# Query and key projections on sixteen 32x32 tiles of TensorE, and another order of work within each mLSTM head

## The chip, the cores and the metric

One core of a Trainium2 chip. The metric is the device time of one execution of the whole program, in microseconds (us). 1% is some 20 us.

## The reference, cut to what matters

Two decoder layers for a prompt of 512 tokens and 64 sample tokens (8 sequences of 8). Layer 0 mixes with an RG-LRU, layer 1 with an mLSTM, and each is followed by a SwiGLU and a gated input embedding. Only the mLSTM's heads are touched. For each of 4 heads of width 512:

```
q = block_diag(xc, w_q); k = block_diag(xc, w_k) * 512 ** -0.5; v = block_diag(xm, w_v)    # blocks of 4x4
S   = (q k^T) * exp(decay, causal)
num = inter * (q C) + S v ;  den = inter * (q n) + sum(S) ;  h = num / max(|den|, exp(-m))
C_new = scale * C + kw^T v ;  n_new = scale * n + sum(kw)       # C is 512x512 for each head and sequence
h = rms_norm(h) ; y = (sigmoid(o_pre) * h) @ w_out
```

C of the 8 sample sequences is read and written once for each head: 8 MB in and 8 MB out.

## The kernel before, in words

Most of the program is the function `job` (L2105): weights of 256x256 are loaded (SP), split in two halves of precision (ACT L929, POOL L634) and multiplied on TensorE (L2125). Between the mLSTM's input and output products lies the stage of the heads, without any `job`, where this change is made.

Everything in that stage is written out by hand: each engine has its own list of steps, and semaphores join them. TensorE's pieces and the PSUM bank of each are listed in `head_order` (L71); `take` (L2252) waits on TensorE until the last user of a bank has emptied it, `done` counts pieces. The engines run their lists strictly in order.

The pieces of one head on TensorE:
- `projection` (L2284, L2288): q and k of the prompt, 4 fp32 products each of 128x128 weights, which are block-diagonal in blocks of 4, with 512 columns. Each takes one bank, which ACT copies out (L1235, L1241). `sample_projection` (L2296): the same for 64 sample tokens, pieces `qs` and `ks`.
- `value` (L2281), pieces `v0` to `v4`; `value_stack` (L2305, `vs`) and `sample_key_rows` (L2326, `st`): rows of v and k, for the updates of C.
- `unit(h, u)`, u from 0 to 7: for 4 sequences and 128 rows of C, q C on four column tiles of 128x32 (L2376), then the update's product on four row tiles of 32x128 (L2386) into banks 4 to 7. DVE's `update` (L1917, L1924) adds it to C in place, and SP stores that. The loop on SP (L566) stores half a unit, and then loads one six halves ahead, as soon as the store before has landed; six halves of C have room.
- the scores `sc0`, `sc13`, `sc2s` (L2340, L2362), the key rows `r0` to `r3` (L2334), `weighted` `pv0` to `pv3` (L2398), `den` and `ds` (L2407 to L2418), `prompt_state` `cp0` to `cp3` (L2426), the square sums `hp` of the prompt and `hn` of the samples (L2454).
- `numerators` (L2429): `cn`, 4 products with one column, and `nt`, 12 products with 32 or 64 columns (L2443, L2445).

In heads 1 to 3 the order before is: qs, ks, vs, v0, hn of the head before, v1, v2, st, v3, v4, q, unit 0, k, unit 1, sc0, unit 2, sc13, sc2s, unit 3, r0 to r3, unit 4, pv0, pv1, unit 5, pv2, pv3, unit 6, den, ds, cp0, cp1, unit 7, hp, cp2, cp3, cn, nt.

The rows with the decay of head h+1 are spread over all partitions by five transfers (`spread_rows`, L546), which SP issues after the store of v = 13, that is the second half of unit 6. DVE turns them into exponents (`decay_exponents(h+1)`, L1862) after `update(h, 7)`, waiting for the transfers, and ACT takes the exponential (`exps_`, L1279) ahead of emptying cp2, cp3, cn and nt. `inverses` (L1959) is DVE's reciprocal. After head 3, ACT starts to split the weights of the next `job`, and SP issues them after all stores of the heads.

## Time and profile before

| | us |
|---|---|
| median of 3 runs | 2048.03 |
| lowest and highest | 2043.64, 2049.47 |
| the profiled execution, its own time | 2048.11 |
| its span, first to last instruction | 2046.4 |

2048.11 - 2046.4 = 1.7 us lie around the span. TensorE is busy for 95% of the span. The granted clock of TensorE was 0.968 of 2.4 GHz on average; it has two levels, 2.4 and 1.2 GHz, and a clock of 0.50 in a row means 1.2. Each fp32 product appears as two records of MATMUL, and each lasts longer than its step to the next, since they overlap: a step is read from one start to the next.

### The profile page before, as it was taken

The page shows a single profiled execution, that of the slowest core. Times are in us where ns is not written, and L with a number is a line of the kernel's source. Part 1 is how long each engine was busy: PE and PEld are TensorE (multiplying, and loading weights), DVE is VectorE, ACT ScalarE, POOL GpSimd, SP SyncE. Part 2 cuts the span into 40 slices and gives each one's busy share as a digit, 9 for nine tenths or more (in the row PEclk, how much of TensorE's full clock was granted, in tenths as well). Part 3 has the DMA queues.
Part 4 walks back from the last instruction along what each step waited for, and adds up shares of the span by engine and source line. Part 5 has one row for each costly group of instructions (what it writes and reads, how often), then busy time and mean ns, then how long its engine had stood idle before and what let it go on. Part 6 is the DMA issues. An engine that isn't in the chain of part 4 may idle for free.

```text
span 2046.4 us, 35519 instructions
## 1 busy us (share of the span) xinstructions
PE 1943.5 (95%) x13511; PEld 1798.8 (88%) x13511; DVE 722.6 (35%) x848; ACT 736.4 (36%) x1086; POOL 811.3 (40%) x659
## 2 busy tenths in 40 slices
PE   6999899999999989899889999999999999999997
PEld 5999899999999989897454665799999999999996
DVE  5677622111111122676646466421222111111213
ACT  3576633322222234434242334241443312212332
POOL 4243364553553545562100100263655545545432
PEclk7999899999999999999879889899999999999998
DMA  3232132222222223221649467322233222222212
GB/s 110 72 93 78 57 99 78 82 83 83 82 82 83 82 68 76 81 82 62 227 142 306 164 237 231 129 89 72 72 89 86 83 89 75 82 90 76 84 60 74
DMA packets 187003, 209.43 MB, mean 102 GB/s; under 512 B 24459, under 2 KB 150035, under 8 KB 186847
## 3 DMA queue, kind: packets, MB, share of 16 engines
q1 hardware_dynamic: 186250, 207.41, 32.8%
q8 instruction: 70, 1.15, 0.2%
q10 hardware_dynamic: 648, 0.59, 0.1%
q14 instruction: 35, 0.29, 0.0%
HBM read 167.31 MB, written 40.64 MB: 102 GB/s over the span
## 4 chain that ended last, share of the span: by engine, by line
PE 75%; DMA 6%; issue 6%; DVE 5%; POOL 4%; ACT 3%; ACTq 0%; SPq 0%; POOLq 0%; DVEq 0%
PE ps L2125 64%; DMA out_ml_C_s_dram<-C_HALVES 4%; POOL W_LO L634 3%; PE ps L2426 2%; DMA C_HALVES<-in_state_mlstm_C_dram 1%; PE ps L2281 1%; POOL SQUARE_SUM L642 1%; PE ps L2288 1%; DVE H_PAD L1641 1%; DVE C_HALVES L1924 1%; PE ps L2305 1%; PE ps L2376 1%; PE ps L2445 1%; PE ps L2296 1%; PE ps L2407 0%
## 5 line engine op out<-in xcount | busy, mean ns | idle before, releaser
L634 POOL TENSOR_TENSOR W_LO<-W_RAW,W_HI 128x512 fp32r<-128x512 f32 x464 | 608.8, 1322 | 709.2 <-ACT W_HI L929 708.9
L929 ACT ACTIVATE W_HI<-W_RAW 128x512 fp32r<-128x512 f32 x484 | 297.9, 628 | 729.1 <-PE ps L2125 723.1
L2125 PE MATMUL ps<-A_HI,W_HI 128*128 128x288 f32 x2304 | 497.3, 298 | 14.8 <-POOL W_LO L634 6.2
L2125 PE MATMUL ps<-A_LO,W_HI 128*128 128x288 f32 x2304 | 495.6, 297 | 0.0
L2125 PE MATMUL ps<-A_HI,W_LO 128*128 128x288 f32 x2304 | 494.9, 297 | 0.0
L2125 PEld LDWEIGHTS ps<-A_HI,W_HI 128*128 128x128 f32 x2304 | 373.2, 190 | 17.6 <-issue 13.7
L2125 PEld LDWEIGHTS ps<-A_LO,W_HI 128*128 128x128 f32 x2304 | 373.4, 190 | 0.0
L2125 PEld LDWEIGHTS ps<-A_HI,W_LO 128*128 128x128 f32 x2304 | 373.1, 190 | 0.0
L1692 DVE TENSOR_TENSOR X<-X,ps 128x1152 f32 (+1 forms) x36 | 48.7, 1354 | 340.0 <-PE ps L2125 340.0
L2125 PE MATMUL ps<-G_HI,W_HI 128*128 128x288 f32 x704 | 151.0, 296 | 2.4 <-POOL G_LO L743 2.4
L2125 PE MATMUL ps<-G_LO,W_HI 128*128 128x288 f32 x704 | 150.8, 296 | 0.0
L2125 PE MATMUL ps<-G_HI,W_LO 128*128 128x288 f32 x704 | 150.7, 296 | 0.0
L1716 DVE TENSOR_TENSOR GATED<-ps,GATE 128x1152 f32<-128x1152 f32 x22 | 29.9, 1357 | 255.0 <-PE ps L2125 255.0
L2125 PE MATMUL ps<-B_HI,W_HI 128*128 128x288 f32 x512 | 110.8, 298 | 7.2 <-POOL W_LO L634 5.1
L2125 PEld LDWEIGHTS ps<-G_HI,W_HI 128*128 128x128 f32 x704 | 113.4, 189 | 2.9 <-POOL G_LO L743 2.9
L2125 PEld LDWEIGHTS ps<-G_HI,W_LO 128*128 128x128 f32 x704 | 113.4, 189 | 0.0
L2125 PEld LDWEIGHTS ps<-G_LO,W_HI 128*128 128x128 f32 x704 | 113.4, 189 | 0.0
L2125 PE MATMUL ps<-B_HI,W_LO 128*128 128x288 f32 x512 | 110.3, 297 | 0.0
L2125 PE MATMUL ps<-B_LO,W_HI 128*128 128x288 f32 x512 | 110.1, 297 | 0.0
L1711 DVE TENSOR_TENSOR GATE<-ps,RSTD 128x1152 f32<-128x1152 f32 x22 | 29.9, 1358 | 197.6 <-PE ps L2125 197.2
L2125 PEld LDWEIGHTS ps<-B_HI,W_HI 128*128 128x128 f32 x512 | 83.1, 190 | 8.2 <-POOL W_LO L634 5.8
L642 POOL TENSOR_TENSOR SQUARE_SUM<-SQUARE_SUM,SQUARES 128x1152 f32<-128x1152 f32 x20 | 58.3, 2916 | 68.2 <-ACT SQUARES L951 44.8
(374 smaller groups left out, 2450.7 us busy)
## 6 DMA issues: line engine op xcount, KB each, us to landing
W_RAW<-in_ffn_w_up_dram SPq DMA_DIRECT2D x176, 256.0 KB, 2.8
C_HALVES<-in_state_mlstm_C_dram SPq DMA_DIRECT2D x64, 512.0 KB, 5.5
out_ml_C_s_dram<-C_HALVES SPq DMA_DIRECT2D x64, 512.0 KB, 6.2
W_RAW<-in_ffn_w_down_dram SPq DMA_DIRECT2D x88, 256.0 KB, 2.7
...
```

The source lines that it names most:

```text
L634: pool.tensor_tensor(W_LO[:, s], W_RAW[:, s], W_HI[:, s].bitcast(F32), ALU.subtract).then_inc(lo_ready, 1)
L642: pool.tensor_tensor(SQUARE_SUM[:, :, :], SQUARE_SUM[:, :, :], SQUARES[:, :, :], ALU.add).then_inc(acc_ready, 1)
L929: act.activation(W_HI[:, s], W_RAW[:, s], ACT.Copy).then_inc(hi_ready, 1)
L1641: ins = dve.tensor_tensor_scan(H_PAD[:, m, :], A_PAD[:, m, :], U_PAD[:, m, :], 0.0, ALU.mult, ALU.add)
L1692: dve.tensor_tensor(xx, xx, psum4(s), ALU.add).then_inc(psum_freed[s], 1)
L1711: dve.tensor_tensor(pair5(GATE[:, :, :]), psv[:, 0, :, :, 0:HALF_T], RB, ALU.mult).then_inc(psum_freed[0], 1)
L1716: link(dve.tensor_tensor(pair5(GATED[:, :, :]), psv[:, 1, :, :, 0:HALF_T], pair5(GATE[:, :, :]), ALU.mult))
L1924: dve.scalar_tensor_tensor(c, c, old_w(h)[:, DEC_S * b + DEC_S - 1:DEC_S * b + DEC_S], ps[:, 4 + j, :], ALU.mult, ALU.add)\
L2125: ins = pe.matmul(ps[:, 4 * s + 2 * m + h, 0:HALF_T], a[:, w, k, wc], x[:, h * HALF_T:h * HALF_T + HALF_T], start=i == 0 and k == 0 and q ...
L2281: ins = pe.matmul(ps[0:n, bank, c * P:c * P + P], XM[:, 4 * h + c, t0:t0 + n], QKV_DIAG[:, 2, c, :], start=True, stop=True)
L2288: done(h, f"{name}{c}", pe.matmul(ps[:, bank, :], QKV_DIAG[:, "qk".index(name), c, :], XC[:, 4 * h + c, 0:SEQ], start=True, stop=True))
L2426: ins = pe.matmul(ps[:, bank, :], K_WEIGHTED[:, i, kc * P:kc * P + P], V_ROWS[:, i, :], start=i == 0, stop=i == 3)
```

## The change

- q and k of the prompt: `projection` puts the 4 products on 16 tiles of 32x32, row group j and column group c, one for each 32 columns of each weight matrix, all into banks 4 to 7. Features lie permuted in Q_T and K_T, and `key_rows` puts them back. ACT empties q, DVE empties k (in head 0 DVE both).
- The order of the pieces in a head: see the diff. Unit 0 comes after sc0, and the units stand among the other products up to unit 7, after which only cn and cp3 with nt between its four products are left.
- `spread_rows` is issued after v = 11 (unit 5), and `decay_exponents(h+1)` stands ahead of `update(h, 6)`.
- The copies of k for `st` go from ACT to POOL. In head 0 the rows of the gates are worked out in another order, with an exponential ahead of them.

Left out below are new buffer places, the removed order of TensorE (it is printed above), and steps of head 0 on DVE and ACT.

```diff
 def head_order(h):
 
+    tail = [("u2", UNIT_BANKS), ("pv2", (1,)), ("pv3", (2,)), ("n0", (0,)), ("u3", UNIT_BANKS), ("den", (3,)), ("ds", (1,)),
+            ("u4", UNIT_BANKS), ("cp0", (2,)), ("hp", (3,)), ("u5", UNIT_BANKS), ("cp1", (1,)), ("u6", UNIT_BANKS), ("cp2", (2,)),
+            ("n1", (0,)), ("u7", UNIT_BANKS), ("cn", (3,)), ("cp3", (1,)), ("nt", (3,))]
     if h == 0:
...
+        return [("v0", (4,)), ("v1", (5,)), ("v2", (6,)), ("v3", (7,)), ("v4", (0,)), ("qt", UNIT_BANKS), ("gates", (2, 3)),
+                ("qs", (1,)), ("gate_rows", (2, 3)), ("ks", (0,)), ("kt", UNIT_BANKS), ("sc0", (2,)), ("st", (4, 5)), ("sc13", (3,)),
+                ("cols", (0,)), ("sel0", (6,)), ("sel2", (7,)), ("vs", (4, 5)), ("sc2s", (1,)), ("sel1", (0,)), ("u0", UNIT_BANKS),
+                ("r0", (2,)), ("r1", (3,)), ("r2", (1,)), ("r3", (2,)), ("pv0", (3,)), ("u1", UNIT_BANKS), ("pv1", (1,))] \
+            + [(name, {"pv2": (2,), "pv3": (3,), "den": (1,), "ds": (2,), "cp0": (3,), "hp": (1,), "cp1": (2,), "cp2": (3,), "cn": (1,),
+                       "cp3": (2,), "nt": (1,)}.get(name, banks)) for name, banks in tail]
+    return [("qt", UNIT_BANKS), ("qs", (0,)), ("ks", (1,)), ("v0", (2,)), ("v1", (3,)), ("kt", UNIT_BANKS), ("vs", (0, 1)), ("v2", (2,)),
+            ("hn", (3,)), ("st", (4, 5)), ("v3", (2,)), ("v4", (3,)), ("sc0", (1,)), ("u0", UNIT_BANKS), ("sc13", (2,)), ("sc2s", (3,)),
+            ("u1", UNIT_BANKS), ("r0", (1,)), ("r1", (2,)), ("r2", (3,)), ("r3", (1,)), ("pv0", (2,)), ("pv1", (3,))] + tail
 
 
 PIECES = [(h - 1 if name == "hn" else h, name, banks) for h in range(HEADS) for name, banks in head_order(h)] + [(HEADS - 1, "hn", (4,))]
 BANKS = {(h, name): banks for h, name, banks in PIECES}
 DONE = {(h, name): i + 1 for i, (h, name, _) in enumerate(PIECES)}
...
+DIAG_USED = [max(DONE[h, name] for name in ("v4", "qt", "qs", "kt", "ks", "vs")) for h in range(HEADS)]
...
-                    if v == 13 and h + 1 < HEADS:
+                    if v == 11 and h + 1 < HEADS:
                         spread_rows(h + 1)
...
+            def key_tokens(h):
+
+                bank = at(h, "ks")
+                pool.wait_ge(bank_freed[bank], FREED[h, "ks", bank])
+                for g in range(2):
+                    t0 = SEQ + g * GROUP_T
+                    for c in range(4):
+                        ins = pool.tensor_copy(
+                            K_TOKENS[:, g, c, :].rearrange("p (j r t) -> p j r t", j=4, r=4),
+                            K_T[:, c, t0:t0 + GROUP_T].rearrange("p (j t) -> p j t", j=4).unsqueeze(2).broadcast_to([P, 4, 4, DEC_S]))
+                ins.then_inc(k_stack_in, 1)
+
...
                 act.wait_ge(piece_done, DONE[h, "cn"])
                 act.activation(N_PROMPT[:, h, :], ps[:, bank, 0:4], ACT.Copy).then_inc(bank_freed[bank], 1)
+                prompt_state(h, 3)
                 bank = at(h, "nt")
                 act.wait_ge(piece_done, DONE[h, "nt"])
...
-            key(0, 0)
-            key(0, 1)
+                act.activation(SUMS[:, hf * HALF_T:hf * HALF_T + HALF_T], ps[:, 2 + hf, 0:HALF_T], ACT.Copy).then_inc(gate_sums, 1)
+            link(act.activation(ABS_F[:, 0:P], IDENT[0:HEADS, :], ACT.Exp))
...
+                    query(h, 0)
+                    query(h, 1)
+                    sample_columns(h, "ks", K_T)
                     sample_columns(h, "qs", Q_T)
+                    query(h, 2)
+                    query(h, 3)
+                    value(h, 0)
+                    value(h, 1)
                     value_stack(h)
                     value(h, 2)
                     key_stack(h)
                     value(h, 3)
                     value(h, 4)
+                    root_mean(h - 1, "hn", SEQ, N_STOK)
...
+                weighted_keys(h)
+                if h == HEADS - 1:
+                    gains(2)
+                for v in range(4):
+                    prompt_values(h, v)
+                sample_values(h, 0)
+                squares(h)
+                if h == HEADS - 1:
+                    gains(3)
+                prompt_state(h, 0)
+                prompt_state(h, 1)
+                root_mean(h, "hp", 0, SEQ)
                 prompt_state(h, 2)
+                sample_values(h, 1)
+                if h + 1 < HEADS:
+                    exps_(h + 1)
                 sample_end(h)
...
             for h in range(HEADS):
                 if h == 0:
                     decay_exponents(0)
+                    v_stack_lo(0)
                     old_queries(0)
...
                     first_scores(0)
                     more_scores(0)
...
+                    update(0, 0)
+                    old_sums(0)
+                    update(0, 1)
                 else:
+                    for c in range(4):
+                        key(h, c)
+                    add_squares(h - 1, N_Q[:, :, :], squares_s, sums_s)
+                    old_queries(h)
                     v_stack_lo(h)
...
                     square_mean(h - 1, "hn", 0, SEQ, N_STOK)
...
                     k_stack_lo(h)
+                    first_scores(h)
+                    update(h, 0)
+                    more_scores(h)
+                    update(h, 1)
+                    old_sums(h)
                     normalise(h - 1, SEQ, N_STOK, 2 * h)
...
                     if h == HEADS - 1:
                         xn_lo(0, G_MIX + 8, A_HI, A_LO)
...
+                update(h, 2)
+                key_sums(h)
+                update(h, 3)
+                add_squares(h, Q_T[:, :, 0:SEQ], squares_p, sums_p)
+                denominators(h)
+                update(h, 4)
+                inverses()
+                update(h, 5)
+                dve.wait_ge(dve_step, step.now())
+                square_mean(h, "hp", 0, 0, SEQ)
                 if h + 1 < HEADS:
                     decay_exponents(h + 1)
                 else:
+                    xn_lo(2, G_MIX + 8, A_HI, A_LO)
+                update(h, 6)
+                if h == HEADS - 1:
                     xn_lo(4, G_MIX + 8, A_HI, A_LO)
+                update(h, 7)
+                if h == HEADS - 1:
                     xn_lo(6, G_MIX + 8, A_HI, A_LO)
                 normalise(h, 0, SEQ, 2 * h + 1)
...
-            def projection(h, name, c):
-
-                bank = at(h, f"{name}{c}")
-                take(h, f"{name}{c}")
-                done(h, f"{name}{c}", pe.matmul(ps[:, bank, :], QKV_DIAG[:, "qk".index(name), c, :], XC[:, 4 * h + c, 0:SEQ], start=True, stop=True))
+            def projection(h, name):
+
+                if h:
+                    pe.wait_ge(wbd_ready, h + 1)
+                take(h, f"{name}t")
+                for c in range(4):
+                    for j in range(4):
+                        rows = slice(32 * j, 32 * j + 32)
+                        ins = pe.matmul(ps[32 * c:32 * c + 32, UNIT_BANKS[j], :], QKV_DIAG[rows, "qk".index(name), c, rows], XC[rows, 4 * h + c, 0:SEQ],
+                                        start=True, stop=True)
+                done(h, f"{name}t", ins)
...
+                for j in range(4):
+                    ins = pe.transpose(ps[:, bank, :].rearrange("p (c j x) -> p j c x", c=4, j=4)[:, j], K_T[:, j, i * P:i * P + P], IDENT[:, :])
                 done(h, f"r{i}", ins)
...
+            def state_and_numerators(h):
+
+                bank, nbank = at(h, "cp3"), at(h, "nt")
+                take(h, "cp3")
                 own = IDENT[:, :].rearrange("p (j x) -> p j x", j=4)[:, :, 0:DEC_S]
                 for v in range(4):
+                    ins = pe.matmul(ps[:, bank, :], K_WEIGHTED[:, v, 3 * P:4 * P], V_ROWS[:, v, :], start=v == 0, stop=v == 3)
+                    if v == 3:
+                        done(h, "cp3", ins)
+                    if v == 0:
+                        take(h, "nt")
+                        pe.wait_ge(bank_freed[0], FREED[h, "n1", 0])
                     c0 = v * N_STOK
+                    pe.matmul(ps[:, nbank, c0:c0 + N_STOK], V_ROWS[0:N_STOK, 4, v * P:v * P + P], own_probs[h % 2], start=True, stop=False, skip_group_check=True)
                     for g in range(2):
+                        ins = pe.matmul(ps[:, nbank, c0 + g * GROUP_T:c0 + g * GROUP_T + GROUP_T], NUM_ROWS[:, g, v * P:v * P + P], own,
                                         start=False, stop=g == 1, skip_group_check=True)
                 done(h, "nt", ins)
...
+            projection(0, "q")
             done(0, "gates", gates(XC, 0, (12,), xc_silu))
...
+            sample_projection(0, "q")
             take(0, "gate_rows")
             pe.wait_ge(gate_sel, 1)
+            pe.wait_ge(gate_sums, 2)
             for hf in range(2):
                 ins = pe.matmul(ps[0:36, 2 + hf, 0:HALF_T], GATE_SEL[:, :], SUMS[:, hf * HALF_T:hf * HALF_T + HALF_T], start=True, stop=True)
             done(0, "gate_rows", ins)
...
             sample_projection(0, "k")
...
+            projection(0, "k")
             first_scores(0)
...
+            sample_key_rows(0)
+            scores_13(0)
             take(0, "cols")
             pe.wait_ge(rows_ready, 1)
             for i, (t0, n) in enumerate(TOKEN_TILES):
...
             for g in range(2):
                 ins = pe.transpose(ps[:, 0, 40 + 4 * g:44 + 4 * g], KEY_W_STACK[:, g, :], IDENT[0:4, 0:4])
             done(0, "cols", ins)
...
+            broadcast("sel0", MAX_ROW)
+            sample_broadcasts()
             value_stack(0)
...
+            scores_2s(0)
+            broadcast("sel1", EXP_ROW)
+            for h in range(HEADS):
+                if h == 0:
+                    unit(0, 0)
+                    for i in range(4):
+                        key_rows(0, i)
+                    weighted(0, 0)
+                    unit(0, 1)
+                    weighted(0, 1)
+                else:
+                    projection(h, "q")
+                    sample_projection(h, "q")
+                    sample_projection(h, "k")
+                    value(h, 0)
+                    value(h, 1)
+                    projection(h, "k")
+                    value_stack(h)
+                    value(h, 2)
+                    square_sum(h - 1, "hn", 0, N_STOK, N_Q[:, 0, :], sums_s)
+                    sample_key_rows(h)
+                    value(h, 3)
+                    value(h, 4)
+                    first_scores(h)
+                    unit(h, 0)
+                    scores_13(h)
+                    scores_2s(h)
+                    unit(h, 1)
+                    for i in range(4):
+                        key_rows(h, i)
+                    weighted(h, 0)
+                    weighted(h, 1)
                 unit(h, 2)
...
                 weighted(h, 2)
                 weighted(h, 3)
+                unit(h, 3)
+                denominators(h)
+                unit(h, 4)
+                prompt_state(h, 0)
+                prompt_squares(h)
+                unit(h, 5)
+                prompt_state(h, 1)
                 unit(h, 6)
...
+                prompt_state(h, 2)
                 unit(h, 7)
...
+                prompt_sums(h)
+                state_and_numerators(h)
 ```

## Rows read from the trace of the kernel before

**Rows 1.** Windows view by stage: us, busy (count) of each engine, PEclk, DMA share, GB/s.
```profile
1046.40:1132.40 86.00, 80.75 (x384) 49.66 (x384) 49.11 (x80) 28.87 (x51) 6.93 (x16) 0.92 0.66 215
1132.40:1216.80 84.40, 79.90 (x383) 48.89 (x384) 49.03 (x80) 28.75 (x51) 6.92 (x16) 0.92 0.65 219
1216.80:1301.80 85.00, 80.43 (x383) 49.26 (x383) 53.12 (x83) 31.62 (x56) 0.00 (x0) 0.92 0.56 187
```
**Rows 2.** The same view, of two stretches at the low clock.
```profile
1009.90:1016.70 6.80, 6.80 (x21) 2.62 (x21) 5.15 (x11) 0.00 (x0) 0.00 (x0) 0.50 0.98 309
1037.20:1054.30 17.10, 14.24 (x61) 13.58 (x62) 7.55 (x9) 6.43 (x19) 1.97 (x5) 0.50 0.40 129
```
**Rows 3.** Timeline of TensorE, start of head 2: start, us, what, records, [idle before].
```profile
1132.37 3.65 PE L2296 MATMUL ps<-XM_XC,QKV_DIAG 128*128 128x64 f32 x16
1135.82 3.73 PE L2305 MATMUL ps<-QKV_DIAG,V_TOKENS 128*128 128x128 f32 x16
...
1153.27 1.06 PE L2376 MATMUL ps<-C_HALVES,Q_OLD 128*32 128x512 f32 x8
...
1154.70 3.70 PE L2288 MATMUL ps<-XM_XC,QKV_DIAG 128*128 128x512 f32 x8
```
**Rows 4.** Timeline of TensorE: pieces at 2.4 GHz, heads 0 and 1.
```profile
942.26 4.86 PE L2281 MATMUL ps<-QKV_DIAG,XM_XC 128*128 128x128 f32 x40
...
958.91 1.00 PE L2296 MATMUL ps<-XM_XC,QKV_DIAG 128*128 128x64 f32 x8
...
1078.87 5.47 PE L2340 MATMUL ps<-Q_T,K_T 128*128 128x384 f32 x24
...
1086.31 2.09 PE L2334 MATMUL ps<-IDENT,K_T 128*128 128x128 f32 x16
...
1090.78 4.58 PE L2398 MATMUL ps<-PROBS,V_ROWS 128*128 128x512 f32 x16
...
1104.86 2.42 PE L2407 MATMUL ps<-PROBS,ONES 128*128 128x512 f32 x8
...
1110.27 7.11 PE L2426 MATMUL ps<-V_ROWS,K_WEIGHTED 128*128 128x512 f32 x16
...
1127.46 0.43 PE L2443 MATMUL ps<-RG_STATE_IN,V_ROWS 64*128 64x64 f32 x2
...
1128.38 0.43 PE L2443 MATMUL ps<-RG_STATE_IN,V_ROWS 64*128 64x64 f32 x2
```
**Rows 5.** Timeline of TensorE: pieces at 1.2 GHz, head 0.
```profile
1010.42 1.94 PE L2376 MATMUL ps<-C_HALVES,Q_OLD 128*32 128x512 f32 x8
...
1040.06 0.69 PE L2443 MATMUL ps<-PROBS_S,V_ROWS 64*128 64x64 f32 x2 [6.31 <-ACT C_PROMPT L1315]
...
1046.36 3.65 PE L2296 MATMUL ps<-XM_XC,QKV_DIAG 128*128 128x64 f32 x16
```
**Rows 6.** Timeline of DVE, end of head 1.
```profile
1111.88 3.75 DVE L1961 RECIPROCAL SQUARE_SUM<-SQUARE_SUM 128x576 f32<-128x576 f32 x1
...
1118.87 2.72 DVE L1924 SCALAR_TENSOR_TENSOR C_HALVES<-C_HALVES,RG_STATE_IN,ps 128x512 f32<-128x512 f32 x4 [2.45 <-PE ps L2386]
...
1122.47 0.88 DVE L1875 TENSOR_SCALAR PROBS<-PROBS,KEY_COLS 128x384 f32<-128x384 f32 x3 [0.28 <-DMA SAMPLE_ROWS<-rows_kept]
...
1124.07 3.33 DVE L1855 RECIPROCAL SQUARES<-SQUARES 128x512 f32<-128x512 f32 x1
```
**Rows 7.** Timeline of SP's queue, heads 0 and 1.
```profile
986.41 2.04 SPq L535 DMA_DIRECT2D out_ml_C_s_dram<-C_HALVES  x2
...
1028.86 0.43 SPq L552 DMA_DIRECT2D PROBS<-rows_kept  x1
...
1115.22 0.48 SPq L552 DMA_DIRECT2D PROBS<-rows_kept  x1
...
1123.59 0.37 SPq L525 DMA_DIRECT2D C_HALVES<-in_state_mlstm_C_dram  x1
```
**Rows 8.** Timeline of TensorE, the first `job` after head 3.
```profile
1304.73 0.82 PE L2125 MATMUL ps<-A_HI,W_HI 128*128 128x288 f32 x2 [2.92 <-POOL W_LO L634]
```

281 lines of the change are left out of this document (63 added, 218 removed), and 4 rows, old and new, of the table OUT_AHEAD.

## The prediction

> **What bounds the kernel now.** I read the windows by stage first: in heads 1 to 3 TensorE is busy 80 of 84 to 86 us, DVE 49 to 53, DMA 0.56 to 0.66 of its time [rows 1]. So a head is TensorE's list, and what is saved there shortens the program. The profiled execution took 2048.11 us, 0.1 from the median of the runs, and the sum below is made against it. What a measurement can tell from no change is some 0.3%, 6.1 us.
>
> Then the timeline of TensorE. A head costs its columns and a surcharge at its border: nt, the sample products and the value stack stand together, and the granted clock falls: four projections of 512 columns take 3.7 us at full clock, while 16 records of 64 columns take 3.45 us from start to start and 16 of 128 columns 3.7, at half [rows 3]. At full clock 8 records of 64 columns take 1.0, some 0.85 without the overlap, and 40 of 128 columns 4.8, 0.12 each [rows 4]. In head 0 the clock was 0.50 from the idle stretch ahead of nt (6.31 us) through nt and the sample products until the value stack was through [rows 2, 5]. Last the queues of DVE and SP, since the change moves steps past waits there.
>
> **The projections.** Removed per head: two blocks of 3.7 us, 3.6 without the overlap [rows 3]. Added: two blocks of 16 tiles. No row has 32x32 tiles. The nearest is the four column tiles of a unit: 8 records, 2 for each product, in 1.06 us, where one after the other they would be 3.7 [rows 3]. If all 16 run side by side, a block costs the same, 1.1; this I take, as four row groups also run side by side in the unit's second half: the whole unit is 1.43 from start to start [rows 3]. Both ends: 1.0, and 16 products one after the other, 16 x 0.9 = 14 us. In between, row groups that take turns: 4 x 1.0. Gain: 2 x 2.5 = 5 us a head. The Trainium skill (TensorE: Matmul & The Clock Gate, the part on packing small matmuls) gives 10.6 times for 16 tiles against one after the other, measured in another type; by it a block would be 14 / 10.6 = 1.3 us, an estimate, and the sum would be 2 us larger. Against the change speaks a rule in TensorEngine Tiling (PSUM Bottleneck): faster tiles leave the emptying of PSUM as the bound. Here ACT's four copies and two smaller ones (under 4 us, if one is like DVE's pass of 0.7) lie beside qs, ks, v0 and v1 on TensorE, 3.6 at full clock and 7 at half, so by the rule 0.4 us could be added at full clock and nothing at half.
>
> **The wait that is moved.** In the new order DVE works through update 5, decay_exponents(h+1), update 6; unit 7's second half needs the banks that update 6 frees. decay waits for the spread rows, and SP issues those only after it has stored both halves of unit 5 and the store before the last has landed. From rows: an update that starts at 1118.87 has SP's load behind its second store at 1123.59, so the first spread would go out 5.2 us after the update's start [rows 6, 7]. From the first spread's issue to decay's start were 1122.47 - 1115.22 = 7.2 us, decay took 1.6, and an update 2.7 [rows 6, 7]. Together 16.8 us from the start of update 5 to the banks of unit 7.
>
> TensorE's own way there is shorter. Steps at full clock [rows 3, 4]: unit 1.43, sc13 with sc2s 6.0 (1078.87 to 1086.31 without the unit in between), r0 to r3 2.05, two pv 4.55, den with ds 5.4, one cp 3.5, hp, a single product of 512 columns, 1.0. From unit 0's start to the end of ds: 4 units 5.7 + 6.0 + 2.05 + 9.1 + 5.4 = 28.3. From there unit 4, cp0, hp, unit 5, cp1, unit 6, cp2, and unit 7's first half: 3 x 1.43 + 3 x 3.5 + 1.0 + 1.0 = 16.8. DVE starts update 5 at 28.3 + 2.2 (denominators: two passes of 0.7 and four small ones of 0.2, an estimate) + 2.7 (update 4) + 4.5 (inverses, the reciprocal being 3.75 [rows 6]) = 37.7, and frees the banks at 37.7 + 16.8 = 54.5. TensorE is there at 28.3 + 16.8 = 45.1. **It stands 9.4 us**, in heads 0 to 2. Behind that wait are queued cn, cp3, nt and the whole next head, and ACT's exponential of the decay, which only POOL's mask waits for.
>
> **The clock behind it.** 6.3 us of idle were followed by half clock in head 0 [rows 2, 5], so 9.4 will be too. What comes then is cn (1.0), cp3 and nt. nt was 6.3 us at half clock (1040.06 to 1046.36) [rows 5] and would be 4 x 0.92 = 3.7 at full [rows 4]; cp3 6.9 instead of 3.5. Whether big products between small sums bring the clock back no row shows. The nearest: it stayed at 0.50 in 1009.9 to 1016.7, a stretch of a unit and the first half of cp0 without a gap [rows 2], and through nt and qs, ks. I take half clock to the end of nt and through qt (1.9, as a unit's first half at half clock [rows 5]), qs, ks (3.45), v0 and v1 (3.5), as the value stack raised it before.
>
> **One of heads 1 and 2**, from nt's end to nt's end. Opening: 1.9 + 3.45 + 3.5, then at full clock kt 1.1, vs 1.9, v2 0.95, hn and the wait for DVE's sums behind four key copies 1.1, st 0.9, v3 and v4 1.9, sc0 3.6: 20.3. To unit 7's second half 54.5; that half 0.8 at half clock, cn 1.0, cp3 and nt 13.2. Sum 89.8, against 86.0 and 84.4 [rows 1]: **+3.8 and +5.4**.
>
> **Head 0.** Its opening is a chain through the gates' rows on ACT and DVE, which is hardly shorter; I take its first store 2 us earlier (bounds 0 and 4). From there it goes by the transfers, which are busy for 0.98 [rows 2]. From the first store to the spread were 42.4 us for 13 halves, 3.3 each [rows 7]; two halves less are 35.9. Spread at 984.4 + 35.9 = 1020.3, decay 1027.5, the banks at 1031.8, nt's end at + 0.8 + 1.0 + 13.2 = 1046.8 against 1046.36 [rows 5]: **+0.4**.
>
> **Head 3** has no spread. Between update 5 and 6 stand one pass of 0.7 and xn_lo, four passes over 576 columns, some 3.0 where an update's four over 512 are 2.7, so unit 7's banks are free at 37.7 + 2.7 + 3.7 + 2.7 = 46.8, 1.7 late. No clock is lost: 20.3 + 46.8 + 0.4 + 0.9 + 3.5 + 3.7 = 75.6 against 85.0 [rows 1]: **-9.4**.
>
> **The restart.** TensorE stood 2.9 us for the first split weights [rows 8]. Now cp3's bank is freed only when nt is almost done, and SP issues the weights behind the store of it, so that their landing is waited for too. The nearest row of an issue that is waited for is the spread's 7.2 us; weights are one transfer and not five, but two splits follow: I take 6.5, **+3.6** (bounds 0, if they land as early as now, and +5).
>
> The other edits I cost at nothing: the key tokens go to POOL, busy for 7 of 86 us [rows 1], and are hidden by v0, v1, kt and vs (without them st would wait some 2 us a head); the permuted transposes have as many columns as before.
>
> Sum: 0.4 + 3.8 + 5.4 - 9.4 + 3.6 = **+3.8 us, 2052**, 0.2% and so within what can't be told from none. The gain of the projections (20 us) and of the borders goes into three waits and the clock behind them.
>
> **The rivals.**
> 1. *The clock comes back inside cp3 with nt.* Then nt and cp3 are 7.2 to 9 instead of 13.2, and qt to v1 4.7 instead of 8.9, at three borders: 3 x 8.5 = 26 us less, 2026. For it: half of that stretch is work of 512 columns. Against: rows 2. Chance 0.2.
> 2. *No wait at unit 7*, because the rows land far sooner than 7.2 us. Heads 1 and 2 then cost 12.1 + 3.6 to unit 0, 45.1, and 8.5 behind it, 69.3; with head 0 some 14 less and head 3 4.6 less: about 1992. Against: the 7.2 us of head 1, of which DVE even waited the last 0.28 [rows 6]. Chance 0.07.
> 3. *Slower: the tiles do not run together.* If the row groups of a column group take turns, a block is 4.0, eight of them cost 8 x 2.9 = 23 more: 2075; one after the other, 8 x 12.6 = 100 more, 2150. In each head the blocks stand on TensorE's path, ahead of the wait and not beside it. It decides from blocks of 1.4 us on, 0.3 over mine, where the sum passes 2054. The change then doesn't do what it says. For it: the trace has row groups side by side and column groups side by side, and never both. Chance 0.1.
> My own case has 0.6; 0.03 is for the rest.
>
> **The numbers.** My case has its terms within 6 us either way (restart 2, head 0 2, wait 1 and clock 1 at each border): of its 0.6, 0.05 faster, 0.31 the same, 0.24 slower. Rivals 1 and 2 give 0.27 faster, rival 3 0.1 slower. With the rest: faster 0.34, same 0.32, slower 0.34. The case's own range is 2046 to 2059. The range from 2024 to 2066 takes in rival 1 and leaves out rivals 2 and 3.
>
> **What would show it.** Right: two blocks of 32 records and 1.1 to 1.3 us in each head; a wait of 9 us at L2386 of unit 7, ended by DVE's update; decay on DVE waiting for the rows of the next head; PEclk 0.50 from there into v1 of the next head; head periods of 90, 90 and 76. Wrong: a clock of 1.00 in nt, blocks over 1.4 us, or a wait at unit 7 under 5.

## The result, and the profile after the change

The changed kernel takes **2057.87 us** (median of 10 runs, 2054.90 to 2065.84), the kernel before beside it 2047.07 us (10 runs, 2041.90 to 2055.09). The ratio is 1.0057, with a 95% interval of 1.0038 to 1.0077: slower by 0.6%, so by more than the 0.3% that was taken as no change. The forecast of 2052 us was 0.3% low; the measured time lies in the range, and in the likeliest case's own range of 2046 to 2059. The profiled execution took 2062.03 us for a span of 2060.3, 13.9 more than the span of before (2046.4), and nearly all of that lies in the head stage (defined below).

The windows by stage, now of heads 1 to 3 of the changed kernel (from one Q block to the next, the last to the end of the numerators); they answer to [rows 1]:

```profile
1054.38:1145.89 91.51, 82.38 (x432) 47.52 (x431) 50.97 (x84) 24.23 (x39) 8.84 (x24) 0.84 0.60 202
1145.89:1236.21 90.32, 82.64 (x432) 47.35 (x431) 50.97 (x84) 24.11 (x39) 8.84 (x24) 0.82 0.61 205
1236.21:1312.80 76.59, 75.94 (x431) 43.92 (x430) 52.80 (x84) 26.74 (x44) 1.94 (x8) 0.92 0.59 199
```

Two heads are 5.5 and 5.9 us longer than before, the last is 8.4 us shorter. TensorE's busy time in heads 1 and 2 has grown by 1.6 and 2.7 us, although the tiles take 5 us of work at the full clock out of each: the granted clock is 0.84 and 0.82 where it was 0.92. The waits of TensorE in the head stage say where it starts:

```profile
PE ps L2381 <- DVE C_HALVES L1916: 23.7, 3, 8.9
PE ps L2110 <- POOL W_LO L631: 5.9, 1, 5.9
PE ps L2332 <- DVE K_T L1782: 3.0, 1, 3.0
```

L2381 is the second half of a unit; the three waits are those of unit 7 in heads 0 to 2, of 8.95, 7.71 and 7.08 us. The timeline of TensorE at the end of head 1 and the start of head 2 has the second of them and all that is queued behind it:

```profile
1129.42 0.80 PE L2381 MATMUL ps<-V_STACK,KW_STACK 32*128 32x512 f32 x4 [7.71 <-DVE C_HALVES L1916]
1130.15 1.87 PE L2430 MATMUL ps<-ONES,SUMS 128*128 128x1 f32 x8
1131.88 2.05 PE L2439 MATMUL ps<-V_ROWS,K_WEIGHTED 128*128 128x512 f32 x2
...
1145.89 2.01 PE L2277 MATMUL ps<-XM_XC,QKV_DIAG 32*32 32x512 f32 x32
1147.83 3.67 PE L2287 MATMUL ps<-XM_XC,QKV_DIAG 128*128 128x64 f32 x16
1151.30 3.06 PE L2266 MATMUL ps<-QKV_DIAG,XM_XC 128*128 128x128 f32 x16
1154.29 1.14 PE L2277 MATMUL ps<-XM_XC,QKV_DIAG 32*32 32x512 f32 x32
1155.36 2.05 PE L2296 MATMUL ps<-QKV_DIAG,V_TOKENS 128*128 128x128 f32 x16
```

The clock is low as soon as the wait ends: the four records of unit 7's second half take 0.80 us, where 0.51 are usual. A product of 512 columns (two records) takes 2.05 us, which is half clock, through cp3 and the numerators (14.0 us), Q's block (2.01), the sample products and into the values. K's block is the first piece wholly at the full clock here: sixteen tiles, 32 records, in 1.14 us. The windows view gives the clock from the end of the wait on, in heads 0 and 1:

```profile
1037.90:1065.00 27.10, 27.09 (x140) 16.94 (x140) 9.42 (x10) 5.49 (x12) 2.66 (x11) 0.50 0.56 188
1129.40:1153.50 24.10, 24.08 (x102) 15.45 (x103) 9.42 (x10) 4.44 (x11) 2.25 (x10) 0.50 0.62 211
```

DVE's timeline says why the bank is late, and SP's queue why DVE is:

```profile
1112.52 2.71 DVE L1916 SCALAR_TENSOR_TENSOR C_HALVES<-C_HALVES,RG_STATE_IN,ps 128x512 f32<-128x512 f32 x4
1115.15 0.68 DVE L1836 TENSOR_TENSOR SQUARES<-SQUARES,ps 128x512 f32<-128x512 f32 x1
1124.96 0.88 DVE L1863 TENSOR_SCALAR PROBS<-PROBS,KEY_COLS 128x384 f32<-128x384 f32 x3 [9.12 <-DMA SAMPLE_ROWS<-rows_kept]
...
1126.56 2.71 DVE L1916 SCALAR_TENSOR_TENSOR C_HALVES<-C_HALVES,RG_STATE_IN,ps 128x512 f32<-128x512 f32 x4
```
```profile
1118.53 0.48 SPq L549 DMA_DIRECT2D PROBS<-rows_kept  x1
```

The update of unit 5 starts at 1112.52, the spread rows are issued at 1118.53, DVE goes on at 1124.96 with the exponents, and the update of unit 6, whose banks unit 7 needs, at 1126.56.

At the restart, the first job after the heads:

```profile
1318.70 0.82 PE L2110 MATMUL ps<-A_HI,W_HI 128*128 128x288 f32 x2 [5.86 <-POOL W_LO L631]
```

It starts 13.97 us later than in [rows 8], after 5.86 us of idle time in place of 2.92.

The clock also fell where TensorE had not waited at all, for a short stretch behind the 4-column products that end `ds`. In head 3 the next large piece, cp0, took 5.40 us where 3.70 are full clock (5.27 in head 0, 4.54 in head 2, 3.70 in head 1):

```profile
1283.31 1.90 PE L2413 MATMUL ps<-RG_STATE_IN,KW_STACK 128*128 128x4 f32 x16
...
1286.57 5.40 PE L2421 MATMUL ps<-V_ROWS,K_WEIGHTED 128*128 128x512 f32 x8
```

Below, **the head stage** is counted from the start of the first values (40 records, 942.26 in [rows 4], 942.52 after) to that first job: 362.5 us before, 376.2 after. It leaves out the stages ahead of it, whose length differs between the profiled runs: the first values start between 940.33 and 945.82 us.

### The profile page after: what moved, and what is told of

Same layout as the page of the kernel before. It is cut to its first block, busy times and chain, and to the rows that moved or that the text cites. A ratio compares the mean times of both kernels' runs of the same rounds, so it can differ in the third digit from the quotient of the medians.

```text
span 2060.3 us, 35924 instructions
## 1 busy us (share of the span) xinstructions
PE 1947.2 (95%) x13703; PEld 1790.9 (87%) x13703; DVE 731.4 (35%) x863; ACT 719.3 (35%) x1040; POOL 825.3 (40%) x691
## 4 chain that ended last, share of the span: by engine, by line
PE 76%; issue 6%; DVE 5%; POOL 4%; DMA 3%; ACT 3%; SPq 0%; ACTq 0%; POOLq 0%; DVEq 0%
PE ps L2110 64%; POOL W_LO L631 3%; DMA out_ml_C_s_dram<-C_HALVES 2%; PE ps L2393 1%; PE ps L2332 1%; PE ps L2439 1%; PE ps L2371 1%; PE ps L2266 1%; POOL SQUARE_SUM L639 1%; DVE C_HALVES L1916 1%; DVE H_PAD L1622 1%; PE ps L2448 1%; PE ps L2421 1%; PE ps L2277 1%; PE ps L2381 1%
## 5 line engine op out<-in xcount | busy, mean ns | idle before, releaser
L631 POOL TENSOR_TENSOR W_LO<-W_RAW,W_HI 128x512 fp32r<-128x512 f32 x464 | 609.7, 1324 | 691.2 <-ACT W_HI L941 690.9
L2110 PE MATMUL ps<-A_HI,W_HI 128*128 128x288 f32 x2304 | 497.9, 298 | 17.7 <-POOL W_LO L631 9.2
L2110 PE MATMUL ps<-A_LO,W_HI 128*128 128x288 f32 x2304 | 495.5, 297 | 0.0
L2110 PE MATMUL ps<-A_HI,W_LO 128*128 128x288 f32 x2304 | 494.9, 297 | 0.0
L2110 PEld LDWEIGHTS ps<-A_HI,W_HI 128*128 128x128 f32 x2304 | 373.5, 190 | 20.6 <-issue 16.6
L2110 PEld LDWEIGHTS ps<-A_LO,W_HI 128*128 128x128 f32 x2304 | 373.4, 190 | 0.0
L2110 PEld LDWEIGHTS ps<-A_HI,W_LO 128*128 128x128 f32 x2304 | 373.3, 190 | 0.0
L2110 PE MATMUL ps<-G_HI,W_HI 128*128 128x288 f32 x704 | 151.0, 296 | 2.5 <-POOL G_LO L740 2.5
L2110 PE MATMUL ps<-G_LO,W_HI 128*128 128x288 f32 x704 | 150.7, 296 | 0.0
L2110 PE MATMUL ps<-G_HI,W_LO 128*128 128x288 f32 x704 | 150.7, 296 | 0.0
L2110 PE MATMUL ps<-B_HI,W_HI 128*128 128x288 f32 x512 | 110.7, 298 | 6.8 <-POOL W_LO L631 4.7
L2110 PEld LDWEIGHTS ps<-G_HI,W_HI 128*128 128x128 f32 x704 | 113.4, 189 | 2.9 <-POOL G_LO L740 2.9
L2110 PEld LDWEIGHTS ps<-G_HI,W_LO 128*128 128x128 f32 x704 | 113.5, 189 | 0.0
L2110 PEld LDWEIGHTS ps<-G_LO,W_HI 128*128 128x128 f32 x704 | 113.5, 189 | 0.0
L2110 PE MATMUL ps<-B_LO,W_HI 128*128 128x288 f32 x512 | 110.0, 297 | 0.0
L2110 PE MATMUL ps<-B_HI,W_LO 128*128 128x288 f32 x512 | 110.0, 297 | 0.0
L2110 PEld LDWEIGHTS ps<-B_HI,W_HI 128*128 128x128 f32 x512 | 82.8, 190 | 7.9 <-POOL W_LO L631 5.2
```

The source lines that it names most:

```text
L631: pool.tensor_tensor(W_LO[:, s], W_RAW[:, s], W_HI[:, s].bitcast(F32), ALU.subtract).then_inc(lo_ready, 1)
L2110: ins = pe.matmul(ps[:, 4 * s + 2 * m + h, 0:HALF_T], a[:, w, k, wc], x[:, h * HALF_T:h * HALF_T + HALF_T], start=i == 0 and k == 0 and q ...
```

## The experiments

### What the tiles are worth here

```
 for c in range(4):
-    for j in range(4):
-        rows = slice(32 * j, 32 * j + 32)
-        ins = pe.matmul(ps[32 * c:32 * c + 32, UNIT_BANKS[j], :], QKV_DIAG[rows, "qk".index(name), c, rows], XC[rows, 4 * h + c, 0:SEQ],
-                        start=True, stop=True)
+    ins = pe.matmul(ps[:, UNIT_BANKS[c], :], QKV_DIAG[:, "qk".index(name), c, :], XC[:, 4 * h + c, 0:SEQ],
+                    start=True, stop=True)
...
```

`key_rows` transposes the features in their natural order again, with as many columns.

> The changed kernel with each projection of Q and of K as four 128x128 products again (features in their natural order, key rows transposed accordingly), everything else as changed. Theory (tiles are worth what their rows say): at the full clock four products cost about 3.4 us against 1.15, in heads 1 to 3 Q's block lies at half clock, about 6.8 against 2.0; the sum over eight blocks is 2 x 2.3 in head 0 and 3 x (2.3 + 4.8) later, about +25 us of TensorE, and as TensorE ends the head stage nearly all of it shows: +15 to +26 us against the changed kernel. Rival (tiles off the path): K's block is covered by the copies of Q's banks, and the time moves by less than 8 us. In both the waits at unit 7's second half stay at 7 to 9 us.

2073.92 us (2067.88 to 2077.92), ratio to before 1.0125 (1.0089 to 1.0161): 16 us more than the changed kernel; the head stage 13.8 us longer. In the theory's span at its low end, and not as it was reckoned. The timeline of TensorE at the start of head 2 in this kernel:

```profile
1153.60 6.41 PE L2275 MATMUL ps<-XM_XC,QKV_DIAG 128*128 128x512 f32 x8
1159.84 1.90 PE L2285 MATMUL ps<-XM_XC,QKV_DIAG 128*128 128x64 f32 x16
```

Q's block, four long products, takes 6.41 us where the tiles take 2.01, but the sample products behind it take 1.90 us where they took 3.67. The clock came back inside the block, and so it did in heads 1 and 3, where the block took 5.08 and 6.26 us; with tiles it was still low behind Q's block in all three. From the start of Q's block to that of K's are 8.63, 9.96 and 9.81 us in heads 1, 2 and 3, against 9.06, 8.40 and 9.06 with tiles. So where the clock is low the tiles gain -0.4, 1.6 and 0.8 us for Q, and not the 4.8 that the expectation reckoned: the short block is followed by more work at half clock. What brings the clock back sooner behind the long products, no run takes apart. K's block takes 3.5 us from start to start, against 1.66, 1.07 and 1.20 with tiles, a gain of 1.9 to 2.4. Together that is 1.4, 4.0 and 3.1 us a head.

The short fall of the clock behind the 4-column products is here too, without any tiles, in all four heads (cp0 takes 5.00, 4.04, 5.25 and 5.11 us); in head 2:

```profile
1203.80 1.90 PE L2411 MATMUL ps<-RG_STATE_IN,KW_STACK 128*128 128x4 f32 x16
...
1207.15 5.25 PE L2419 MATMUL ps<-V_ROWS,K_WEIGHTED 128*128 128x512 f32 x8
```

### Spread rows issued earlier

```
-if v == 11 and h + 1 < HEADS:
+if v == 7 and h + 1 < HEADS:
     spread_rows(h + 1)
```

> The changed kernel with one edit: SyncE issues the next head's spread rows after the store of half 7 instead of half 11, nothing else. Theory (the spread rows make the wait at unit 7, and the wait makes the half clock): the waits of 8.95, 7.71 and 7.08 us fall to under 1.5 us each (about -20 us), the clock stays high from unit 7 over the end of the head to the next Q block (about 14.0 us becomes 7.5 us per border, then some 3 more; about -28 us), together -40 to -55 us: about 2005 to 2018 us. Rival A (the clock falls by itself in the small sums of the end of a head): only the wait goes, -15 to -24 us, and the low stretches stay. Rival B (the wait goes elsewhere, to the C halves or to VectorE's work): under -10 us.

2031.57 us (2024.66 to 2043.63), ratio 0.9929 (0.9903 to 0.9955): 26.3 us under the changed kernel, between the theory and rival A. The 23.7 us of waits at L2381 are gone, but the windows of the four head ends, from the key sums to the next Q block (the fourth to the end of the numerators), show three at half clock and one at full:

```profile
1032.34:1048.08 15.74, 15.74 (x44) 9.19 (x40) 9.42 (x10) 3.35 (x5) 1.97 (x5) 0.50 0.86 268
1118.07:1133.38 15.31, 15.31 (x45) 8.76 (x41) 9.42 (x10) 3.64 (x6) 1.97 (x5) 0.52 0.90 287
1202.36:1212.00 9.64, 8.53 (x45) 5.12 (x41) 9.42 (x10) 3.64 (x6) 1.97 (x5) 1.00 0.95 304
1277.61:1293.40 15.79, 15.79 (x44) 9.18 (x40) 10.87 (x12) 0.77 (x2) 0.00 (x0) 0.50 0.27 101
```

And the waits of TensorE in the head stage name a new one:

```profile
PE ps L2371 <- DMA C_HALVES<-in_state_mlstm_C_dram: 9.5, 5, 2.6
```

TensorE now reaches unit 7's first half before its C halves have landed: 2.34, 2.04, 1.03 and 2.60 us in heads 0 to 3. In heads 0, 1 and 3, where it stood 2 us or more, the clock was low behind it (in head 1 only from within cn on); in head 2, where it stood 1.03, it was not. In the changed kernel the waits at this place were under 0.8 us, and DVE's wait stood behind them.

### The wait left as it is, but filled

```
+if u == 7 and h + 1 < HEADS:
+    bank = at(h, "cn")
+    pe.wait_ge(bank_freed[bank], FREED[h, "cn", bank] - 1)
+    for i in range(8):
+        pe.matmul(ps[:, bank, :], K_WEIGHTED[:, i % 4, 0:P], V_ROWS[:, i % 4, :], start=True, stop=True)
 take(h, f"u{u}")
```

> The changed kernel with eight unused 128x128 by 512 products in heads 0 to 2, put between the C part of unit 7 and its second half, so that TensorE works about 6.9 us of the 7.1 to 9 us in which it waited; the wait's end is left as it is. Theory (the idle time brings the clock down): the granted clock stays at 1.0 to the next Q block, and the time falls by 15 to 30 us though nothing was taken off the path. Rival (the small sums at the end of the head bring it down whatever came before): the clock falls a few us later, and the time is unchanged within 5 us.

2026.65 us (2023.25 to 2033.31), ratio 0.9908 (0.9872 to 0.9943): **31 us under the changed kernel, for work added and none taken away**. The timeline of TensorE at the end of head 1:

```profile
1112.83 7.13 PE L2383 MATMUL ps<-V_ROWS,K_WEIGHTED 128*128 128x512 f32 x16
1120.16 0.51 PE L2386 MATMUL ps<-V_STACK,KW_STACK 32*128 32x512 f32 x4 [0.20 <-DVE C_HALVES L1916]
1120.60 1.05 PE L2435 MATMUL ps<-ONES,SUMS 128*128 128x1 f32 x8
...
1129.07 1.14 PE L2277 MATMUL ps<-XM_XC,QKV_DIAG 32*32 32x512 f32 x32
```

Unit 7's second half still waits for DVE (0.59, 0.20 and 0.42 us), after 7.1 us of filling work; from the key sums to the next Q block are 8.47 us and not 15.74, in all three heads. This is the price of the clock by itself: the head stage is 35.4 us shorter, 11.8 a border, and by the medians it is 10.4 a border, in all just over the theory's 15 to 30. It is shown that the idle time brought the clock down in the changed kernel: without it the same small sums did not, at any of the three places.

### Head 0's key tokens back on ScalarE

GpSimd's call is taken out, and ScalarE gets the same copies:

```
 v_stack(0)
-key_tokens(0)
...
 sample_columns(0, "ks", K_T)
+act.wait_ge(bank_freed[at(0, "ks")], FREED[0, "ks", at(0, "ks")])
+for g in range(2):
+    t0 = SEQ + g * GROUP_T
+    for c in range(4):
+        ins = act.activation(
+            K_TOKENS[:, g, c, :].rearrange("p (j r t) -> p j r t", j=4, r=4),
+            K_T[:, c, t0:t0 + GROUP_T].rearrange("p (j t) -> p j t", j=4).unsqueeze(2).broadcast_to([P, 4, 4, DEC_S]), ACT.Copy)
+ins.then_inc(k_stack_in, 1)
 key_stack(0)
```

> The changed kernel with the eight copies that make head 0's key tokens back on ScalarE, ahead of its copy of the transposed keys (GpSimd keeps those of heads 1 to 3). Theory (GpSimd took 5.9 us for them beside VectorE's work on the gate rows, and that made the transposes, ScalarE's exponentials and the first store late): the eight copies take about 2 to 3 us, the first store comes 2 to 4 us earlier, and the time falls by 2 to 4 us. Rival (the gate rows on VectorE decide): the first store and the time stay within 1 us.

2056.68 us (2051.01 to 2060.48; 10 runs), ratio 1.0048 (1.0034 to 1.0062). The 1.2 us under the changed kernel are less than the intervals allow to tell. The trace is clearer: ScalarE makes the eight copies in 1.71 us where GpSimd took 5.93, the first store comes 2.1 us earlier (44.9 us after the first values, against 47.1), and the head stage is 3.2 us shorter.

```profile
962.29 1.71 ACT L1348 ACTIVATE K_TOKENS<-K_T 128x128 f32<-128x128 f32 x8
```

### A short filling ahead of the C halves

The kernel of e2_spread7 with, in a unit:

```
+if u == 7:
+    bank = at(h, "cn")
+    pe.wait_ge(bank_freed[bank], FREED[h, "cn", bank] - 1)
+    for i in range(3):
+        pe.matmul(ps[:, bank, :], K_WEIGHTED[:, i, 0:P], V_ROWS[:, i, :], start=True, stop=True)
 for half in range(2):
     pe.wait_ge(c_loaded[(n + half) % CSLOTS], 16 * ((n + half) // CSLOTS + 1))
```

> The kernel of e2_spread7 (2031.6 us) with three unused 128x128 by 512 products (about 2.6 us at the full clock) in every head ahead of unit 7's wait for its C halves, where that kernel's TensorE stood idle for 2.3, 2.0 and 2.6 us in heads 0, 1 and 3, with the low clock behind each, and not in head 2, with the full clock behind it. Theory (a wait of some 2 us for a C half is enough to bring the clock down ahead of the small sums): the clock stays high at all four head ends, each of the three takes about 6.5 us less up to the next head and some 3 more behind it: -18 to -28 us against e2_spread7, about 2004 to 2014. Rival (head 2 was spared for another reason, the DMA's load or chance): the clock falls as before in heads 0, 1 and 3, and the time is 2030 to 2036.

2039.38 us (2031.18 to 2047.41), ratio 0.9955 (0.9935 to 0.9975). A miss: by the medians 8 us slower than without the filling (the two intervals touch), and nothing gained of the 18 to 28 us; close to the rival, but not for the rival's reason. The timeline of TensorE at the end of head 0:

```profile
1029.71 2.74 PE L2372 MATMUL ps<-V_ROWS,K_WEIGHTED 128*128 128x512 f32 x6
1032.38 1.06 PE L2376 MATMUL ps<-C_HALVES,Q_OLD 128*32 128x512 f32 x8
1033.38 0.51 PE L2386 MATMUL ps<-V_STACK,KW_STACK 32*128 32x512 f32 x4
1033.81 1.05 PE L2435 MATMUL ps<-ONES,SUMS 128*128 128x1 f32 x8
1034.73 1.10 PE L2444 MATMUL ps<-V_ROWS,K_WEIGHTED 128*128 128x512 f32 x2
1036.95 0.69 PE L2451 MATMUL ps<-PROBS_S,V_ROWS 64*128 64x64 f32 x2 [1.12 <-ACT N_PROMPT L1321]
```

The filling did its part: no wait at the C halves, and cn and the first product of cp3 at the full clock. The half clock begins at the next wait, 1.12 us in the first numerators, which need the bank that ScalarE's little copy of the key sums frees; that copy stands behind the next head's exponentials. So it went in heads 0, 1 and 2; head 3, which has no next exponentials, kept the full clock. Whether 1.1 us is enough to cause this is what e9_fill3_exps asks.

### Exponents behind unit 7

On VectorE, and below it on ScalarE:

```
-if h + 1 < HEADS:
-    decay_exponents(h + 1)
 update(h, 6)
...
 update(h, 7)
+if h + 1 < HEADS:
+    decay_exponents(h + 1)
...
-if h + 1 < HEADS:
-    exps_(h + 1)
 sample_end(h)
+if h + 1 < HEADS:
+    exps_(h + 1)
```

> The changed kernel with VectorE's decay exponents of the next head put behind its update of unit 7 (they stood ahead of update 6), and ScalarE's exponentials of them behind the end of the head; SyncE's spread rows stay where the change has them. Theory (the wait is VectorE's, queued behind the spread rows): the waits at unit 7 fall from 7 to 9 us to under 1.5, the clock stays high, and the time falls by 35 to 50 us, to about 2008 to 2022; the exponentials are made beside the next head's projections and cost nothing there. Rival A (unit 7 then waits 2 us for its C half, and the clock falls on that as in e2_spread7): 2025 to 2036. Rival B (the exponentials, late, hold up ScalarE's copies of Q's banks or the first scores): a new wait of 3 to 6 us at the start of a head, which takes the clock with it: 2035 to 2050.

2017.13 us (2011.56 to 2023.16), ratio 0.9860 (0.9823 to 0.9897): 40.7 us under the changed kernel and 30 to 31 under before. The theory holds for the wait and the clock behind it: no wait at unit 7, and from the key sums to the Q block 8.46 us at the full clock:

```profile
1106.39:1114.85 8.46, 8.46 (x44) 5.12 (x40) 8.20 (x11) 1.07 (x3) 0.00 (x0) 1.00 1.03 333
```

Its last part, that the late exponentials cost nothing, does not, and of rival B a part came: K's block waits 1.36 us for the last copy of Q's banks, which stands behind the exponentials, and the clock stayed up.

```profile
1121.12 1.15 PE L2277 MATMUL ps<-XM_XC,QKV_DIAG 32*32 32x512 f32 x32 [1.36 <-ACT Q_T L1247]
```

The head stage is 325.1 us, 51.1 shorter than that of the changed kernel: 23.7 of it the waits, the rest for the most part the clock.

### The restart

```
 store_cp(h, 0)
-store_cp(h, 1)
+if h + 1 < HEADS:
+    store_cp(h, 1)
...
 o_job(0)
+store_cp(HEADS - 1, 1)
```

> The changed kernel with one edit in SyncE's queue: the last store of head 3's prompt state stands behind the weight loads of the first job after the heads, not ahead of them. Theory (the restart waits for SyncE, which waits for ScalarE's copy of the last prompt state, late since the products of it stand among the small sums): the idle time of 5.9 us at the first job falls to about 3, and the time by 2 to 4 us. Rival (the loads wait for the C stores ahead of them, or the half clock behind the wait decides): less than 1 us.

2058.59 us (2051.78 to 2064.78), ratio 1.0051 (1.0030 to 1.0072). The idle time fell as expected:

```profile
1319.35 0.50 PE L2112 MATMUL ps<-A_HI,W_HI 128*128 128x288 f32 x2 [3.13 <-POOL W_LO L633]
```

The head stage is 1.9 us shorter, and the medians don't show it. That the wait comes from SP's order is shown; what it is worth is under what these runs can tell.

### The tiles again, at the full clock

The kernel of e6_late with the edit of e1_plain.

> The kernel of e6_late with the projections as four 128x128 products each: what the tiles are worth where the clock is high. Theory: 2.3 us a block, eight blocks, +14 to +20 us against e6_late. Rival (each Q block is then followed by long products that only the copies of its banks wait for, so it hides): under +8 us.

2027.99 us, from 2014.55 to 2040.31 in 7 runs, ratio 0.9919 (0.9881 to 0.9957). That is 10.9 us over e6_late by the medians, but the intervals overlap, so it is not told from none; the reckoned 14 to 20 is not reached. The profiled run of e8_late_plain is the fastest of its seven, and as fast as that of e6_late (2014.55 and 2014.28 us); its head stage is 5.2 us longer, of which 4.4 lie in head 0. From Q block to Q block heads 1 and 2 take 75.4 and 75.1 us without tiles and 75.1 and 75.1 with them: what the tiles took out there, other things took back. With tiles K's block comes so early that it waits for the copies of Q's banks (1.36 us a head), and in the profiled run with tiles the clock fell for one short stretch behind the 4-column products of the denominators, at no wait, some 3 us a head:

```profile
1083.88 2.21 PE L2413 MATMUL ps<-RG_STATE_IN,KW_STACK 128*128 128x4 f32 x16
1086.02 1.94 PE L2371 MATMUL ps<-C_HALVES,Q_OLD 128*32 128x512 f32 x8
...
1088.61 5.44 PE L2421 MATMUL ps<-V_ROWS,K_WEIGHTED 128*128 128x512 f32 x8
```

In 75 us about each of heads 1 and 2 TensorE was busy 73.1 us at a clock of 0.95 there, and 74.2 us at 1.00 in e8_late_plain. The tiles are not needed for that fall: it stands in all four heads of e6_late, but also in head 0 of e8_late_plain (cp0 5.40 us), in all four of e1_plain, and in head 0 of the kernel before, the first stretch of [rows 2]. There, as in all heads of the new order, a unit follows the 4-column products; in heads 1 to 3 of the kernel before cp0 and cp1 follow them, and the clock stayed high (7.11 us for the two). That this order makes the fall likelier is not tested. The seven executions of e8_late_plain had mean clocks of 0.967 (2040.31 us) to 0.977 (2015.26 us); the profiled one had 0.976.

Against the kernel before, e8_late_plain is 0.8% faster with the same four long products. So by the medians more than half of the 1.4% of e6_late comes without the tiles, from the order of the work.

### The wait of 1.1 us taken away

The kernel of e5_spread7_fill3 with

```
-if h + 1 < HEADS:
-    exps_(h + 1)
 sample_end(h)
+if h + 1 < HEADS:
+    exps_(h + 1)
```

> The kernel of e5_spread7_fill3 (2039.4 us) with ScalarE's exponentials for the next head behind the end of the head instead of ahead of it, nothing else. There TensorE's only wait at a head's end was 1.1 us, in the first numerators, for ScalarE's small copy of the key sums, which stood behind those exponentials; the clock was low behind it in heads 0, 1 and 2. Theory (this wait of 1.1 us among the small sums brought the clock down): without it the clock stays high there, 6 to 7 us less per head up to the next Q block and some 3 more behind it: -20 to -30 us, about 2010 to 2019. Rival (the three added products, or the small sums themselves, bring it down): the clock falls in cp3 and the numerators as before, and the time is 2034 to 2040.

2017.11 us (2014.68 to 2020.58), ratio 0.9856 (0.9831 to 0.9882): 22.3 us less for two calls exchanged on ScalarE. From the key sums to the Q block are 8.47, 8.46 and 8.46 us in heads 0, 1 and 2, where e5_spread7_fill3 had 15.2. Shown: taking the 1.1 us wait away at this place gains 7 to 9 us a head (22.3 us of the medians, 27.8 of the head stages, for three).

### All together

The kernel of e6_late with the edits of e4_actkeys and e7_restart; and that kernel with `exps_(h)` behind `query(h, 3)` of the next head.

> The kernel of e6_late (2017.1 us) with the edits of e4_actkeys and of e7_restart, each of which took 2 to 3 us off the head stage in its trace but not clearly off the medians. Theory: both stand at ends where TensorE waits, so they add: -4 to -7 us, about 2010 to 2013, about 36 us under the kernel before. Rival (the stretches at half clock elsewhere in the head stage move by more than that from run to run): within 3 us of e6_late.

2010.07 us (2003.63 to 2020.34, 6 runs), ratio **0.9822 (0.9793 to 0.9852)**: 37 us under before, 47.8 under the changed kernel. Of e6_late it is 7 us under by the medians, as the theory had it, but the intervals overlap, and the two head stages are equal (325.4 and 325.1 us). The profiled run lost one head end to the clock, behind a wait for the C halves:

```profile
1172.50 1.07 PE L2380 MATMUL ps<-C_HALVES,Q_OLD 128*32 128x512 f32 x8 [1.10 <-DMA C_HALVES<-in_state_mlstm_C_dram]
1173.49 0.51 PE L2390 MATMUL ps<-V_STACK,KW_STACK 32*128 32x512 f32 x4
1173.93 1.27 PE L2439 MATMUL ps<-ONES,SUMS 128*128 128x1 f32 x8
1175.06 2.05 PE L2448 MATMUL ps<-V_ROWS,K_WEIGHTED 128*128 128x512 f32 x2
```

> The kernel of e10_best with ScalarE's exponentials behind its copies of Q's four banks in the next head, not ahead of them. Theory (in e6_late TensorE waited 1.36 us ahead of each K block for the last copy of Q's banks, which stood behind the exponentials): these waits go, -3 to -5 us against e10_best. Rival (the exponentials are then late for GpSimd's masks and key tokens, or for the copies of V): TensorE waits for those 1 us or more, among small products, and the clock goes with it; +3 to +15 us.

2014.70 us (1999.97 to 2020.62, 6 runs), ratio 0.9835 (0.9807 to 0.9864); no difference from e10_best can be told, so neither the theory's gain nor the rival's loss. The waits of 1.36 us are gone and three of 1.6 us have come, the first half of the rival; behind the one in head 1 the clock was low for some 3 us, behind the other two it was not:

```profile
1121.45 1.06 PE L2326 MATMUL ps<-IDENT,K_TOKENS 128*128 128x128 f32 x8 [1.59 <-POOL K_TOKENS L870]
```

A single run of these kernels is no measure of them: e10_best's six lie between 2003.63 us at a mean clock of 0.976 and 2020.34 at 0.967, in the order of their clocks.

## Why the prediction was right, and where it was not

**The shape held.** The step that the forecast rested on, the wait at unit 7's second half, was foreseen with its place, its releaser and its size: 9.4 us in heads 0 to 2, measured 8.95, 7.71 and 7.08. The end of the wait came as reckoned (54.0 and 54.1 us from the start of unit 0 in heads 1 and 2, forecast 54.5); TensorE was there 1.2 and 1.9 us later than the 45.1 reckoned, so the wait was shorter and the time the same. Filling the wait and taking it away (e3_filler, e6_late) show that it and the clock behind it are more than the whole loss: 51 us of head stage hang on it.

**The projections.** 1.1 us a block was taken; 1.14 to 1.16 were measured at the full clock and 2.01 at half. The estimate of 1.3 from the Trainium skill's 10.6 times (TensorE: Matmul & The Clock Gate, packing small matmuls) was too high; the trace decides for 1.15. Rival 3 is out (its far end, 14 us a block, would have added 8 x 12.9 = 103 us and not 100, which changes nothing). The gain of 5 us a head was right for two blocks at the full clock. Behind the low clock e1_plain shows 1.4, 4.0 and 3.1 us in heads 1 to 3, since the clock comes back sooner there with the long products. In the changed kernel no projection waited for a bank. In e6_late, where the stalls are gone, K's block waits 1.36 us for ScalarE's copies out of Q's banks. The rule of the Trainium skill (TensorEngine Tiling (Array Packing), PSUM Bottleneck), that behind faster tiles the copies out of PSUM may become the bound, agrees with that in part: with the exponentials behind the same copies (e11_best_q) that wait is gone, so the copies bound only with what stood ahead of them in ScalarE's queue.

**Half clock to the end of the numerators and into the values.** Right, and rival 1 wrong: with half of that stretch big products, the clock stayed at 0.50 for 24 to 27 us. But the sizes were a little small: cn 1.87 and not 1.0 (it was priced at the full clock though it stands behind the wait), cp3 with the numerators 14.0 and not 13.2. That is 1.5 us a border.

**Heads 1 and 2**: +5.5 and +5.9, forecast +3.8 and +5.4. By its parts head 2 was 19.8 + 54.1 + 16.5 us; the working had 20.3 + 54.5 + 15.0, so the error at its end was in part made up ahead of it. **Head 3**: -8.4, forecast -9.4; "No clock is lost" was wrong there, since cp0 alone lost 1.7 us to the clock that fell behind the 4-column products. That fall was in the kernel before too, in the stretch of [rows 2] that the prediction read only for how long the clock stays low.

**Head 0 is the step that failed**: "I take its first store 2 us earlier (bounds 0 and 4)", and with it +0.4 for the head. It was +8.0. The first store came at 989.58, 3.2 us later than before, outside both bounds; the 11 halves up to the spread took 36.9 us where 35.9 were taken; the tail took 1.5 more. Of the 5.2 us by which the store missed the forecast, e4_actkeys shows 2.1 to be the key tokens' move to GpSimd, which the prediction costed at nothing. It looked at GpSimd's busy share and at heads 1 to 3, not at what waits for these copies in head 0:

```profile
962.76 5.93 POOL L868 COPY K_TOKENS<-K_T 128x128 f32<-128x128 f32 x8 [21.14 <-ACT K_T L1253]
...
1151.99 1.94 POOL L868 COPY K_TOKENS<-K_T 128x128 f32<-128x128 f32 x8 [21.85 <-ACT K_T L1253]
```

The same eight copies take 1.94 us in head 2, where DVE stands idle, and 5.93 in head 0, beside DVE's work on the gate rows (busy 5.69 of the 5.93 us). In the changed kernel key_stack, ScalarE's exponentials and the rows that the first unit needs stand behind them. The other 3 us are not settled: the order of that opening was changed in many places at once, and it was not taken apart. The runs only bound it. Counted from the first values, the first store comes at 44.2 us before, at 47.1 in the changed kernel and at 50.9 in e1_plain, which has the long products of before. So the tiles bring it 3.9 us forward, and the rest of the change puts it 6.8 us back, of which the key tokens are some 2.

**The restart**: idle 5.86 us against 2.92, +2.9, forecast +3.6, by the mechanism given (e7_restart).

The sum was +3.8; the measured terms add to 8.0 + 5.5 + 5.9 - 8.4 + 2.9 = +13.9, which is the span's. Head 0 makes 7.6 of the 10.1 us between them. The case was right, its range held the time, and its 2052 stood 2 us from the bound of slower; with head 0 sized right it would have said slower.

**Rival 2** (no wait, 1992) was not what happened, but e6_late is that world, made by another edit. Its head stage is 37.4 us shorter than before's, so the price of 56 us was too high: a head takes 75.1 us where 69.3 were reckoned (by the working's own terms its opening was 12.5 and not 12.1 us). The exponentials get in the way of Q's copies, the clock falls behind the 4-column products, and head 0 is late there too (first store at 46.9 us).
